# Forget gate of a hybrid decoder trunk: logits computed transposed and cumulated by a scan on VectorE

## What is computed

```
hdn     = rms_norm(x, norm_g[1])
proj    = hdn @ b_w_in                       # 1024 x (4*1024 + 8)
q,k,v,z = split(proj[..., :4096], 4)
f_logit = proj[..., 4096:] + b_f_bias        # one logit for each token and head
log_f   = log_sigmoid(f_logit)
c       = cumsum(log_f over tokens)
q, k    = rms_norm(q), rms_norm(k)           # by head
scores  = q k^T / sqrt(128) + (c[query] - c[key]), causal, softmax
x       = x + (probs @ v * silu(z)) @ w_out[1]
```

## Time and profile before

| | |
|---|---|
| median of 3 runs | 595.29 us (595.1 to 595.59) |
| the profiled execution, its own time | 596.05 us |
| its span in the profile | 594.3 us |
| mean granted clock of PE | 0.977 |
| PE busy | 579.3 us, 3219 matmuls |
| DVE, ACT, POOL busy | 343.6, 249.1, 267.3 us |
| HBM traffic | 48 MB, 81 GB/s |

### The profile page before, as it was taken

How to read it: one execution, slowest core, us unless ns; L and a number is a source line. 1 busy time by engine, 2 the same in 40 slices (tenths; PEclk the granted TensorE clock), 3 DMA queues, 4 the chain that set the end, 5 groups by cost and what they waited for, 6 DMA issues and landing times.

```text
span 594.3 us, 9968 instructions
## 1 busy us (share of the span) xinstructions
PE 579.3 (97%) x3219; PEld 538.6 (91%) x3219; DVE 343.6 (58%) x825; ACT 249.1 (42%) x759; POOL 267.3 (45%) x318
## 2 busy tenths in 40 slices
PE   5799999999999999999999999999999999999998
PEld 4689999999999999888899799999999999998887
DVE  4946766767685949464640074747473737373721
ACT  5535353536262635242541254445362626351500
POOL 4664554536372827063662053536362627270600
PEclk9899999999999999999996699999999999999999
DMA  9532322223131313024422024422331335131221
GB/s 284 152 106 81 99 66 77 72 71 88 53 88 53 104 38 124 18 72 137 120 70 75 0 72 71 75 69 60 83 88 53 88 53 90 51 107 34 72 89 53
DMA packets 77195, 48.36 MB, mean 81 GB/s; under 512 B 4080, under 2 KB 71408, under 8 KB 77168
## 3 DMA queue, kind: packets, MB, share of 16 engines
q1 hardware_dynamic: 77168, 48.02, 30.1%
HBM read 45.91 MB, written 2.10 MB: 81 GB/s over the span
## 4 chain that ended last, share of the span: by engine, by line
PE 88%; DVE 4%; DMA 3%; SPq 2%; ACT 1%; issue 1%; POOL 1%
PE banks L295 24%; PE banks L297 24%; PE banks L296 24%; PE banks L402 5%; PE banks L387 3%; PE banks L354 2%; DMA w_raw<-in_b_w_in_dram 2%; PE banks L372 2%; PE banks L376 2%; PE banks L371 2%; DMA first_raw<-in_a_w_in_dram 1%; SPq L230 1%; DVE probs L677 1%; PE banks L375 1%; DVE hT_lo L685 1%
## 5 line engine op out<-in xcount | busy, mean ns | idle before, releaser
L959 POOL TENSOR_TENSOR w_lo<-w_raw,w_hi 128x512 fp32r<-128x512 f32 x152 | 193.6, 1302 | 69.3 <-ACT w_hi L524 69.3
L295 PE MATMUL banks<-w_hi,hT_hi 128*128 128x384 f32 x512 | 176.5, 345 | 6.9 <-DVE qkn L740 5.3
L296 PE MATMUL banks<-w_lo,hT_hi 128*128 128x384 f32 x512 | 172.3, 337 | 0.0
L297 PE MATMUL banks<-w_hi,hT_lo 128*128 128x384 f32 x512 | 172.3, 336 | 0.0
L974 POOL TENSOR_TENSOR msq<-ssq,eps 128x2 f32<-128x2 f32 x64 | 13.9, 217 | 206.6 <-ACT junk L551 206.6
L295 PEld LDWEIGHTS banks<-w_hi,hT_hi 128*128 128x128 f32 x512 | 97.2, 190 | 8.1 <-DVE qkn L740 6.0
L524 ACT ACTIVATE w_hi<-w_raw 128x512 fp32r<-128x512 f32 x152 | 87.4, 646 | 24.1 <-DMA w_raw<-in_b_w_in_dram 14.4
L296 PEld LDWEIGHTS banks<-w_lo,hT_hi 128*128 128x128 f32 x512 | 97.0, 190 | 0.0
L297 PEld LDWEIGHTS banks<-w_hi,hT_lo 128*128 128x128 f32 x512 | 96.8, 189 | 0.0
L551 ACT ACTIVATE junk<-banks 128x128 bf16<-128x128 f32 x128 | 34.3, 274 | 121.4 <-PE banks L297 121.4
L818 DVE RECIPROCAL gz<-gz 128x128 f32<-128x128 f32 x64 | 58.1, 930 | 0.5
(11 more groups left out here) (107 smaller groups left out, 931.7 us busy)
## 6 DMA issues: line engine op xcount, KB each, us to landing
w_raw<-in_b_w_in_dram SPq DMA_DIRECT2D x64, 256.0 KB, 3.7
w_raw<-in_a_w_in_dram SPq DMA_DIRECT2D x56, 256.0 KB, 3.0
w_raw<-in_w_out_dram SPq DMA_DIRECT2D x32, 256.0 KB, 2.9
xs<-in_x_dram SPq DMA_DIRECT2D x4, 512.0 KB, 6.6
first_raw<-in_a_w_in_dram SPq DMA_DIRECT2D x8, 256.0 KB, 5.8
out_dram<-xs SPq DMA_DIRECT2D x7, 256.0 KB, 2.1
gz<-in_norm_g_dram SPq DMA_DIRECT2D x2, 512.0 KB, 4.4
cos_t<-in_rope_cos_dram SPq DMA_DIRECT2D x1, 256.0 KB, 5.5
```

Source lines behind the costliest of these rows:

```text
L295: pe.matmul(dst, ah, bh, start=first and m == 0, stop=False)
L296: pe.matmul(dst, ah, bl, start=False, stop=False)
L297: mm = pe.matmul(dst, al, bh, start=False, stop=last and m == n - 1)
L959: pool.tensor_tensor(w_lo[:, slot, k, :], raw, f32(w_hi[:, slot, k, :]), ALU.subtract).then_inc(wlo_set, by)
```

## The change

The operands of the forget matmul change places, and with them the layout of all that follows.

- One tensor `wf` of 40 columns for each chunk: the high parts of the 8 heads in columns 0 to 7, the low parts in 32 to 39, zeros between, cleared by POOL among the first constants. It is the stationary operand; hT_hi and hT_lo with all 512 tokens move. `forget` thus issues 16 matmuls into partitions 0 to 39 of bank 4. Rows 0 to 7 hold the sums with the high weights, rows 32 to 39 those with the low ones (low times low is now included).
- `forget` stands between qkv tiles 1 and 2.
- ACT copies rows 32 to 39 to SBUF, DVE adds both and the bias, now one value for each partition. The steps of log_sigmoid run on [8, 512] between the readings of tiles 2 and 3: |f| on DVE, Exp and Ln (with 1 added in the activation) on ACT, min(f, 0) - ln on DVE. The scratch is sin_t and rot.
- The cumulated sum is one `tensor_tensor_scan` of 512 elements on DVE, state * 1 - log_f, which gives -c. The triangle goes, POOL writes 8x512 ones instead. ACT and DVE split the result into crows; ACT does it before exp_z, not behind it.
- `junk` has two slots instead of four, and `read_qkv` waits for all of ACT's own earlier squares.

```diff
-        wf_hi = sb("wf_hi", [P, KC, HEADS], F32R)
-        wf_lo = sb("wf_lo", [P, KC, HEADS], F32R)
-        fbias = sb("fbias", [P, HEADS])
-        flog = sb("flog", [P, 4, TILES, HEADS])
+        wf = sb("wf", [P, KC, LO_ROW + HEADS], F32R)
+        fbias = sb("fbias", [HEADS, 1])
...
-            def logf():
+            def forget():
                 pe.wait_ge(wf_split, 2)
-                for t in range(TILES):
-                    mm = three(banks[:, LOGF_BANK, t * HEADS:(t + 1) * HEADS],
...
+                pe.wait_ge(hTlo_set, 2 * TILES * LAYERS)
+                pe.wait_ge(pTlo_set, 3 * HEADS)
+                for k in range(KC):
+                    pe.matmul(banks[0:LO_ROW + HEADS, FORGET_BANK, :], wf[:, k, :], hT_hi[:, k, :], start=k == 0, stop=False)
+                    mm = pe.matmul(banks[0:LO_ROW + HEADS, FORGET_BANK, :], wf[:, k, :], hT_lo[:, k, :],
+                                   start=False, stop=k == KC - 1)
                 mm.then_inc(f_done, 1)
-            def cumulate():
...
                     qkv(layer, 0, 0, 0)
                     turn_hidden(layer, TILES - 1)
-                    for t in range(1, TILES):
-                        qkv(layer, 0, 0, t)
-                if layer == 1:
-                    logf()
+                    qkv(layer, 0, 0, 1)
+                    forget()
+                    qkv(layer, 0, 0, 2)
+                    qkv(layer, 0, 0, 3)
                 zproj(layer, 0, 0)
-                if layer == 1:
-                    cumulate()
                 turn_qk(layer, 0)
...
+                    act.wait_ge(f_done, 1)
+                    act.activation(f_lo, banks[LO_ROW:LO_ROW + HEADS, FORGET_BANK, :], ACT.Copy).then_inc(f_act, 1)
+                    read_qkv(layer, 0, 0, 2)
+                    split_w(layer, 1, 1, (4, 5))
+                    act.wait_ge(f_step, 2)
+                    act.activation(f_exp, f_exp, ACT.Exp, scale=-1.0).then_inc(f_act, 1)
+                    act.wait_ge(f_act, 2)
+                    act.activation(f_exp, f_exp, ACT.Ln, bias=1.0).then_inc(f_act, 1)
+                    read_qkv(layer, 0, 0, 3)
                 split_w(layer, 1, 1, (6, 7))
                 if layer == 1:
...
+                    act.wait_ge(f_step, 4)
+                    act.wait_ge(consts_set, 1)
+                    act.activation(crows[0:HEADS, :], f_all, ACT.Copy).then_inc(chi_set, 1)
                 exp_z(layer, 0)
...
+            def forget_logits():
+                dve.wait_ge(f_act, 1)
+                dve.scalar_tensor_tensor(out=f_all, in0=banks[0:HEADS, FORGET_BANK, :], scalar=fbias[:, 0:1], in1=f_lo,
+                                         op0=ALU.add, op1=ALU.add).then_inc(f_step, 1)
                 dve.wait_ge(f_step, 1)
...
+            def cumulate():
+                dve.wait_ge(f_act, 3)
+                dve.scalar_tensor_tensor(out=f_lo, in0=f_all, scalar=0.0, in1=f_exp, op0=ALU.min,
                                          op1=ALU.subtract).then_inc(f_step, 1)
+                dve.wait_ge(f_step, 3)
+                dve.wait_ge(ones_set, 1)
+                dve.tensor_tensor_scan(f_all, ones, f_lo, 0.0, ALU.mult, ALU.subtract).then_inc(f_step, 1)
...
             pool.memset(f32(crows[:, :]), 0.0)
+            pool.memset(f32(wf[:, :, :]), 0.0)
...
-                    pool.memset(tri, 1.0).then_inc(tri_set, 1)
-                    pool.wait_ge(tri_set, 1)
-                    pool.affine_select(out=tri, in_=tri, compare_op=ALU.is_ge, fill=0.0, base=0,
-                                       pattern=[[1, SEQ]], channel_multiplier=-1).then_inc(tri_set, 1)
+                    pool.memset(ones, 1.0).then_inc(ones_set, 1)
```

More of the change, by code:

```diff
@@ L27 @@
 MASKED = -3.0e38
+LO_ROW = 32
 TRI = sum(P * (t + 1) for t in range(TILES))
@@ L118, in build_trunk @@
         tables_set = sem("tables_set")
-        tri_set = sem("tri_set")
+        ones_set = sem("ones_set")
         whi_set = sem("whi_set")
@@ L193, in build_trunk @@
                       (QT_BANK, t, slice(cols.start + CH // 2, cols.stop))]
+        spare = sin_t[:, :, :, :].rearrange("p a b n -> p (a b n)")
+        f_lo, f_all = spare[0:HEADS, 0:SEQ], spare[0:HEADS, SEQ:2 * SEQ]
+        f_exp = rot[:, :, :, :].rearrange("p a b n -> p (a b n)")[0:HEADS, :]
+        ones = cos_t[:, :, :, :].rearrange("p a b n -> p (a b n)")[0:HEADS, SEQ:2 * SEQ]
         def normed(layer, t):
@@ L548, in read_qkv @@
                 wait(act, rstd_set, a - 1)
-                wait(act, ssq_set, a - 1)
+                wait(act, ssq_set, a)
                 for m in range(2):
-                    sq = act.activation(junk[:, 2 * (t % 2) + m, :], banks[:, t % 2, m * P:(m + 1) * P],
+                    sq = act.activation(junk[:, m, :], banks[:, t % 2, m * P:(m + 1) * P],
                                         ACT.Square, scale=SCALE, accum_out=ssq[:, t % 2, m:m + 1])
@@ L612, in first @@
                             act.wait_ge(small_in, 32)
-                            act.activation(wf_hi[:, :, :], wf_raw[:, :, :], ACT.Copy).then_inc(wf_split, 1)
+                            act.activation(wf[:, :, 0:HEADS], wf_raw[:, :, :], ACT.Copy).then_inc(wf_split, 1)
                 else:
@@ L616, in first @@
                     split_hidden(layer, TILES - 1)
-                    for t in range(1, TILES):
-                        split_w(layer, 1, 1, (2 * t - 2, 2 * t - 1))
-                        read_qkv(layer, 0, 0, t)
+                    split_w(layer, 1, 1, (0, 1))
+                    read_qkv(layer, 0, 0, 1)
+                    split_w(layer, 1, 1, (2, 3))
+                    act.wait_ge(f_done, 1)
[7 more added lines that the diff above has]
+                    read_qkv(layer, 0, 0, 3)
                 split_w(layer, 1, 1, (6, 7))
                 if layer == 1:
[L622 to L625, removed]
+                    act.wait_ge(f_step, 4)
+                    act.wait_ge(consts_set, 1)
+                    act.activation(crows[0:HEADS, :], f_all, ACT.Copy).then_inc(chi_set, 1)
                 exp_z(layer, 0)
[L627 to L631, removed]
                 split_qk(layer, 0)
@@ L888, in first @@
                     norm_qk(layer, 0, 0)
[L889 to L892, removed]
+                    split_v(layer, 0, 0, 1)
+                    norm_qk(layer, 0, 1)
+                    forget_logits()
+                    split_v(layer, 0, 0, 2)
+                    norm_qk(layer, 0, 2)
+                    split_v(layer, 0, 0, 3)
+                    norm_qk(layer, 0, 3)
+                    cumulate()
                     dve.wait_ge(consts_set, 1)
                     set_pick(0, 0)
-                if layer == 1:
-                    dve.wait_ge(chi_set, 1)
-                    dve.scalar_tensor_tensor(out=crows[32:32 + HEADS, :], in0=banks[0:HEADS, CUM_BANK, :], scalar=-1.0,
-                                             in1=f32(crows[0:HEADS, :]), op0=ALU.mult,
-                                             op1=ALU.subtract).then_inc(c_set, 1)
+                    split_c()
                 split_qk(layer, 0)
```

34 lines of the change are left out of this document (9 added, 25 removed).

## The result

| | before | changed |
|---|---|---|
| median | 595.19 us (4 runs, 595.04 to 595.59) | 577.4 us (4 runs, 576.71 to 577.65) |
| ratio, 95% interval | | 0.9694 [0.9681, 0.9706] |
| profiled execution, its span | 596.05, 594.3 us | 577.4, 575.6 us |
| mean granted clock of PE | 0.977 | 0.994 |

The forecast was 576.2 us in 574.4 to 579.1. The medians differ by 17.8 us, the profiled executions by 18.65.

A forecast was written before the change was run, and what follows sets the result against it. PE was taken to bound the kernel. The profiled 596.05 us less 19.1 us of PE's stretch gave 576.95; the median, 0.76 lower, gave 576.2 us, range 574.4 to 579.1, chance 0.83.

The forecast's parts named there:

- The low clock belongs to logf: At layer 1's start, the clock falls to 0.50 within logf; without logf, zproj takes 5.47 us instead of 8.16.
- Rival C: Layer 1's low-clock stretch has another cause and comes anyway; only 9.2 us go: 586.1 us, chance 0.01.
- The stretch: PE between the last qkv tile and turn_qk: 19.1 us less (17.85 logf + 2.25 cumulate + 2.69 zproj - 3.7 forget).
- B: The clock falls in forget because 40 of 128 weight columns are too little: 579.8 us, chance 0.05.
- D: DVE's scan carries each result through the whole pipeline before the next element, 97 us: 670 us, chance 0.02.
- the 1.5 kept for the start-up: Allowance of 1.5 us both ways, as a small shift at the start may lengthen or shorten low-clock stretches.
- The median of the runs is 0.76 below the profiled one: Last step of the sum: 576.95 us for a profiled run becomes a median of 576.2 us.
- The side chain: Gate steps on ACT and DVE, from forget to qkT_lo, run beside PE and end 1.9 us before the scores.
- I take 0.7, the row of its own shape: The scan on DVE priced at 0.7 us like the two-input 8x512 operation, between bounds of 0.68 and 3.8 us.
- Rival A: Late side chain: a scan of 3.8 us makes PE wait 1.2 us ahead of the scores: 577.4 us, chance 0.08.
- Table loads: On ACT in the side chain, each load costs 1.28 us, without the drain of about 1380 ns the skill adds.
- Tile 3's reading: Behind ACT's Exp, table load and Ln, reading qkv tile 3, possible at 316.6 us, slips by 0.2 us.

The follow-up runs named there:

- the run with 256 columns: The kernel before with logf's moving operand repeated from 8 to 256 columns, result unchanged: 587.18 us against 595.72, ratio 0.9855.

## Why the prediction was right

**What bounds.** Right: PE before and after, 88% of the chain and then 94%. **The low clock belongs to logf.** Right, and now shown by the run with 256 columns. Rival C fell with it: it would give 586.1 to the changed kernel, which took 577.4 with the clock at 1.00 from forget to turn_qk.

**The stretch.** Forecast 19.1 us less, measured 19.03. Forget 3.7 against 3.72; zproj 5.47 against 5.49; tiles 2 and 3 8.32 against 8.34; the 2.69 us that zproj gives back are there. Rivals B and D fell: the clock held in 64 forget matmuls, and the scan needs 1.2 us / 512 = 2.3 ns an element, not 42.

**From the stretch to the time.** This is where the forecast missed by 1.2 us (576.2 against 577.4). In the profiled execution the miss is 0.45 us, 577.4 against 596.05 - 19.1 = 576.95: 0.07 in the stretch, 0.36 ahead of it, within the 1.5 kept for the start-up. The other 0.76 is the step "The median of the runs is 0.76 below the profiled one", which the sum carried over to the changed kernel. The changed kernel's profiled execution is at its median. The kernel before has one more source of spread, the moment at which the clock falls (26.66 or 28.24 to 28.26 us for one stretch), and it goes with logf. Whether the unprofiled runs of before owe their 0.86 us to it is not shown, since they have no trace.

**The side chain.** The mechanism and the sign of the slack held, its size did not. The step "I take 0.7, the row of its own shape" failed: the scan alone takes 1.19 to 1.21 us. The estimate from the Trainium skill (DVE: opcode table, instruction layouts, handler registers and perf-mode slots, section Datapath and trigger behaviour), half throughput and so 1.2 us, is what was measured. A second thing was missing altogether: I put POOL's w_lo at 318.4 to 320.9 and DVE's cumulate at 319.1 in the same list, and took each at its time alone. The first cost 0.5 us (1.21 against 0.7), the second 1.5 (0.55 + 0.98), together 2.0, more than the 1.9 of slack. PE did not wait only because some 0.4 us came back: DVE started 0.2 us earlier than laid out, the chain behind the scan was 0.1 us shorter, and the scores came 0.1 us later. 0.28 us were left, or 0.11 to the weight load. So the sum stood because of the slack and some luck, not because of the price. Rival A (PE waits 1.2 us at a scan of 3.8) did not come, but was nearer than its 0.08 says.

**Table loads.** The two ACTIVATEs behind a table load start 0.01 to 0.02 us after its 1.28 are over (315.22 to 316.51, 323.39 to 324.69). The drain that the Trainium skill adds (ScalarE: Activation LUTs, section What ACT_TABLE_LOAD costs) does not show. By that page's 1380 ns for each of the two loads the chain would have been an estimated 2.8 us longer, and the slack overdrawn.

**Tile 3's reading** was forecast to start at 316.6 plus a slip of 0.2 us, in a time axis that stood 0.36 earlier: 317.16. It started at 317.05. POOL's pair ended at 321.64, 1.5 us ahead of PE's need at 323.11, not the 1.8 of the forecast (322.7 - 320.9).

**A better version?** None of the runs is shown to beat the changed kernel. That with L850 waiting for POOL has 577.06 us, that with the later memset 577.54, against 577.4 and 577.69; as ratios to the kernel before on their own chips these are 0.9696 and 0.9695 against 0.9694 and 0.9705, within each other's intervals.

## What to carry to other kernels

When a profile shows PE busy with a low granted clock, compare the distance of the starts with the moving columns: many weight loads with few columns behind them cost their loads and, here, the clock of that stretch and of the 5 us behind it. Exchanging the operands took 96 matmuls and 17.85 us to 16 and 3.72; even moving superfluous columns, with nothing exchanged, was 8.5 us faster. An operation that is moved is priced with what runs beside it in its new place, since two-operand VectorE work beside GpSimd's took 1.8 times as long here.

## What was not expected of the hardware

- The granted clock fell to 0.50 in a stretch in which PE shows no idle time at all (15.14 us busy of 15.14). The Trainium skill (TensorE: Matmul & The Clock Gate, section Why this matters for your kernels) names pauses between bursts of matmuls as what costs the clock. The rows speak against reading PE's busy share that way: with 8 and 96 moving columns it fell at 100% busy, with 256 it did not.
- The moment of the fall varied, over the same instructions: 2.71, 2.82 and 4.39 us into logf.
- At 0.50 the distance of two logf starts is 0.21 us instead of 0.11, so the weight loads go by the granted clock too.
- The matmul of 512 columns costs 0.232 us with 40 weight columns and 0.228 with 128 (5.47 / 24): the narrower weight is not cheaper.
